# A list scheduler's costs set to other figures, and one sequence's depthwise convolution moved from VectorE and GpSimd to TensorE

## The chip, the cores and the metric

The kernel runs on the 8 cores of one Trainium2 chip. Each core computes two of the 16 sequences by itself, and the cores exchange nothing. The metric is the device time in microseconds of the slowest core, and the time of a kernel is the median of its runs.

## The reference, cut to what matters

One encoder layer, float32, `x` of (16, 2048, 1024). A pre-RMSNorm and one input projection give q, k, v, and two 512-wide branches `xl` and `gl`. Group A is softmax attention (8 query heads, 2 key/value heads of 64, rotary positions, no mask). Group B is the recurrent block whose first step the change touches:

```python
def centred_depthwise_conv(x, w, b):
    # x (B,S,C), w (CONV_WIDTH, C); taps at offsets -1, 0, +1, +2
    xp = jnp.pad(x, ((0, 0), (1, 2), (0, 0)))
    out = b[None, None, :]
    for j in range(CONV_WIDTH):          # 4 taps
        out = out + xp[:, j:j + S, :] * w[j][None, None, :]
```

The convolved `xc` feeds two block-diagonal gate products for each direction (sigmoids), a decay, and a scan forward and one backward over the 2048 tokens. Their sum times GeLU(`gl`) is the output of group B. Both groups are RMS-normalised, pass one output projection into the residual, and a SwiGLU feed-forward (1024 to 2816 to 1024) follows.

## The kernel before

A core holds everything transposed, channels in the 128 partitions and tokens along the free dimension, mostly in pieces of 512 tokens. The program records operations in streams, one list per purpose, and a list scheduler written in Python (`Prog.order`, lines 107 to 275) then fixes the order of the instructions on every engine. It plays the program through with each operation's `cost` and `lat` (all in us), the `nbytes` of its transfer and the free PSUM banks, and it takes what could start first on an engine. Ties on TensorE go by `pe_rank` (line 1066), and on the other engines a bias is added to the time at which an operation became ready (line 1069). `emit` then writes each engine's list in that order with the semaphore waits. So a `cost` has no effect on how long an instruction takes; it only changes the order. Engines run their lists strictly in order.

The streams of a core, with n = 0, 1 for the sequence:

- A0, A1 (`rec_A`, line 547): four chunks of 512 tokens each. Squares for the norm (line 571, ring `xsq` of 4), the normalised input `uT` (line 582), then 14 projections of 8 matmuls (`mm`, line 483). Query and key blocks have their own norm and rotary steps (lines 605 to 633; the queries leave through the ring `qst` of 4). `xl` and `gl` go through `stg` to the DRAM scratch `xl_d`, `gl_d` (lines 667 and 673).
- C0, C1 (`rec_C`, line 789): for each of 4 channel blocks `cc` and each half `h` of the sequence, `xlp` (one buffer) is loaded from `xl_d` by SyncE (lines 795 and 799). GpSimd makes the first tap with the bias (line 802), VectorE adds the three others (line 807), GpSimd casts to bf16 (line 811). Then gate matmuls, Tanh (line 820), Exp (823), a square on GpSimd (827), two VectorE products (829, 838), Sqrt (833), the scans (843), the sum (852), the product with `gl` (854) and a store to `lr_d`.
- B0, B1 (`rec_B`, line 707): attention in 256 steps for each sequence, each of two 64-row score matmuls (line 731), one Exp over 1024 columns on ScalarE (line 738) and two matmuls with V (line 770). The first `single` steps (`NS0` = 192 for sequence 0, 0 for sequence 1) issue scores one step at a time, the others two steps in one burst. Attention is held back until all of A0 and A1 is issued (line 135).
- D0 to D7: output projection (`d_out`), gate and up products (`d_gu`) and down product (`d_down`, line 1013) for 8 chunks of 512 tokens. The bf16 weights come from DRAM scratch, which the first chunk fills. `wdb` holds two, later four, tiles of w_down of [128, 22, 128] each, loaded at line 908.

PSUM has 8 banks. While attention runs, the scheduler leaves other work two of them (6 and 7), and before that all.

## Time and profile before

| what | value |
|---|---|
| runs of the kernel | 2007.98, 2010.20, 2259.01 us; median 2010.2 us |
| the profiled execution | 2000.34 us |
| span in it, slowest core (core 7) | 1998.8 us; the cores lie from 1983.7 to 1998.8 us |
| TensorE busy | 1785.9 us (89%), 8168 matmuls, mean granted clock 0.951 |
| VectorE busy | 1016.1 us (51%) |
| ScalarE busy | 1098.6 us (55%) |
| GpSimd busy | 350.8 us (18%) |

The busy time of TensorE counts matmuls as they overlap and at the clock that was granted (1.00 is 2.4 GHz, 0.50 is 1.2 GHz), so it isn't the time they would need at full speed. An average over the span hides that the stages have different limits. All times of stretches below are from the first instruction of core 7. "L483 <- ACT L820" is idle time of the engine before an instruction of line 483 that ended when one of line 820 finished.

### The profile page before, as it was taken

To read this page: it belongs to the slowest core of one execution; us is meant where nothing else is said; L and a number is where in the kernel's file an instruction comes from. 1 tells how busy PE (TensorE), PEld (TensorE's weight loads), DVE (VectorE), ACT (ScalarE), POOL (GpSimd) and SP (SyncE) were. 2 spreads that over 40 slices of the span, in tenths; PEclk is the share of its full clock that TensorE was granted. 3 is DMA by queue.
4 is the path that set the end of the run, shared out by engine and by line. 5 is a ranking of instruction groups with operands and counts; after the bars stand their busy time and mean duration, and the time that the engine had idled before them with its cause. 6 is when DMAs were issued, how large, how long until landed. Compare 5 with 4: busy or idle time off the path is not lost.

```text
span 1998.8 us, 24285 instructions; the slowest of 8 cores (1983.7 to 1998.8 us)
## 1 busy us (share of the span) xinstructions
PE 1785.9 (89%) x8168; PEld 714.0 (36%) x8168; DVE 1016.1 (51%) x1249; ACT 1098.6 (55%) x1372; POOL 350.8 (18%) x380
## 2 busy tenths in 40 slices
PE   6995666866769999999999999999999999999997
PEld 2442222311213333333333334444444444444443
DVE  3476999956794232315122253473454634545231
ACT  4678788799988877867677771232113212132010
POOL 2123656454341222100000000000000000000000
PEclk9997768988879999999999999999999999999999
DMA  8655233482318667557533246577486674664632
GB/s 192 190 171 155 95 119 108 129 211 85 98 54 216 135 149 169 133 155 194 152 91 86 85 141 206 162 208 230 142 250 187 189 237 150 196 198 132 215 107 100
DMA packets 139782, 310.97 MB, mean 156 GB/s; under 512 B 18544, under 2 KB 26864, under 8 KB 139664
## 3 DMA queue, kind: packets, MB, share of 16 engines
q1 hardware_dynamic: 111632, 228.55, 38.9%
q0 software_dynamic: 28032, 80.86, 15.7%
q8 instruction: 72, 1.18, 0.2%
q14 instruction: 46, 0.38, 0.1%
HBM read 263.05 MB, written 69.99 MB: 167 GB/s over the span
## 4 chain that ended last, share of the span: by engine, by line
PE 70%; ACT 9%; DVE 9%; DMA 5%; issue 4%; POOL 2%; SPq 0%; DVEq 0%; POOLq 0%; ACTq 0%
PE ps_all L483 56%; PE ps_all L770 9%; PE ps_all L731 5%; ACT arena L738 3%; DVE arena L843 2%; ACT arena L820 2%; DVE arena L807 1%; DMA arena<-q_d 1%; DMA xl_d<-arena 1%; DVE arena L838 1%; DVE arena L582 1%; DMA arena<-w_in 1%; POOL arena L802 1%; DVE arena L829 1%; ACT arena L833 1%
## 5 line engine op out<-in xcount | busy, mean ns | idle before, releaser
L483 PE MATMUL ps_all<-arena 128*128 128x512 bf16 (+1 forms) x6120 | 1462.1, 379 | 138.9 <-ACT arena L820 43.9
L483 PEld LDWEIGHTS ps_all<-arena 128*128 128x128 bf16 x6120 | 595.0, 100 | 860.5 <-issue 255.5
L738 ACT ACTIVATE arena<-ps_all 128x1024 bf16<-128x1024 f32 x512 | 503.2, 1029 | 149.6 <-PE ps_all L731 126.5
L770 PE MATMUL ps_all<-arena 128*65 128x512 bf16 x1024 | 389.7, 400 | 14.6 <-DVE arena L746 11.8
L1004 ACT ACTIVATE arena<-ps_all 128x512 f32<-128x512 f32 x176 | 105.2, 598 | 517.1 <-PE ps_all L483 516.8
L1006 DVE SCALAR_TENSOR_TENSOR arena<-arena,ps_all 128x512 f32<-128x512 f32 x176 | 120.9, 687 | 362.5 <-ACT arena L1004 361.9
L731 PE MATMUL ps_all<-arena 64*128 64x512 bf16 x1024 | 178.5, 395 | 50.3 <-ACT arena L738 46.1
L1027 POOL DMA_DIRECT2D outT<-arena x64 | 34.6, 540 | 1003.4 <-DVE arena L1025 996.6
L1009 DVE SCALAR_TENSOR_TENSOR arena<-arena,ps_all 128x512 bf16<-128x512 f32 x176 | 120.7, 687 | 130.9 <-PE ps_all L483 127.4
L770 PEld LDWEIGHTS ps_all<-arena 128*65 128x65 bf16 x1024 | 108.2, 112 | 211.8 <-issue 155.6
L1025 DVE TENSOR_TENSOR arena<-ps_all,arena 128x512 f32<-128x512 f32 x64 | 43.9, 689 | 154.3 <-PE ps_all L483 154.3
L731 PEld LDWEIGHTS ps_all<-arena 64*128 64x128 bf16 x1024 | 39.7, 94 | 202.8 <-issue 202.8
L827 POOL TENSOR_TENSOR arena<-arena 128x1024 f32<-128x1024 f32 x32 | 83.1, 2598 | 91.0 <-ACT arena L823 77.3
L820 ACT ACTIVATE arena<-ps_all,arena 128x512 f32<-128x512 f32 x128 | 83.7, 708 | 17.0 <-DVE arena L843 11.8
L957 DVE TENSOR_TENSOR arena<-arena 128x512 f32<-128x512 f32 (+1 forms) x104 | 74.7, 719 | 27.6 <-ACT arena L950 21.5
L807 DVE SCALAR_TENSOR_TENSOR arena<-arena 128x1024 f32<-128x1024 f32 x48 | 76.6, 1597 | 19.8 <-POOL arena L802 19.5
L843 DVE TENSOR_TENSOR_SCAN arena<-arena 128x1024 f32<-128x1024 f32 x32 | 82.7, 2599 | 0.1
L982 DVE TENSOR_TENSOR arena<-ps_all,arena 128x512 f32<-128x512 f32 x64 | 43.7, 689 | 57.6 <-PE ps_all L483 57.2
L950 ACT ACTIVATE arena<-arena 128x512 f32<-128x512 f32 x64 | 40.2, 630 | 59.3 <-DVE arena L982 58.6
L746 DVE COPY arena<-ps_all 65x1024 f32<-65x1024 f32 x32 | 38.9, 1217 | 63.5 <-PE ps_all L770 63.5
L829 DVE SCALAR_TENSOR_TENSOR arena<-arena 128x1024 f32<-128x1024 f32 x32 | 45.8, 1434 | 24.0 <-ACT arena L820 24.0
L973 DVE SCALAR_TENSOR_TENSOR arena<-arena 128x512 bf16<-128x512 bf16 x64 | 45.9, 779 | 23.7 <-ACT arena L490 23.6
(59 smaller groups left out, 996.9 us busy)
## 6 DMA issues: line engine op xcount, KB each, us to landing
arena<-wg_s SPq DMA_DIRECT2D x154, 256.0 KB, 3.0
arena<-wu_s SPq DMA_DIRECT2D x154, 256.0 KB, 3.1
arena<-wd_s SPq DMA_DIRECT2D x56, 704.0 KB, 5.4
arena<-xT SPq DMA_DIRECT2D x64, 512.0 KB, 7.5
outT<-arena POOLq DMA_DIRECT2D x64, 256.0 KB, 5.5
arena<-wo_s SPq DMA_DIRECT2D x56, 256.0 KB, 2.7
xl_d<-arena POOLq DMA_DIRECT2D x32, 256.0 KB, 4.6
gl_d<-arena POOLq DMA_DIRECT2D x32, 256.0 KB, 3.5
```

Source lines behind the costliest of these rows:

```text
L483: P.op("pe", lambda e: e.matmul(t.ap(n) if ap is None else ap(t), lhsT=lhsT, rhs=rhs, start=start, stop=stop), reads=reads, writes=[t], co ...
L731: r = e.matmul(T2[i].ap(1024)[:, u * 512:(u + 1) * 512], lhsT=kT[sq][rows, kt:kt + 128], rhs=qb[n % 2][rows, :], start=True, stop=True)
L738: P.op("act", lambda e, i=i, b=b: e.activation(out=Pb[b], in_=T2[i].ap(1024), func=AF.Exp, scale=0.125), reads=[T2[i]], writes=[("Pb", b)] ...
L770: P.op("pe", lambda e, u=u, V=V: e.matmul(O.ap(1024)[0:65, u * 512:(u + 1) * 512], lhsT=V[:, stl, :], rhs=pb[:, u * 512:(u + 1) * 512], st ...
L807: P.op("dve", lambda e, cc=cc, h=h, jj=jj: e.scalar_tensor_tensor(out=xc[h], in0=xlp[:, 2 * h + jj:2 * h + jj + 1024], scalar=col(PR, C_CW ...
L820: P.op("act", lambda e, GT=GT, dst=dst, bc=bc, sm=sm, cc=cc, qs=qs: e.activation(out=dst[:, qs], in_=GT.ap(), func=AF.Tanh, bias=col(DV, b ...
L827: P.op("pool", lambda e, u=u: e.tensor_tensor(out=us[u], in0=ua[u], in1=ua[u], op=ALU.mult), reads=[("ua", u)], writes=[("us", u)], cost=c ...
L843: P.op("dve", lambda e, u=u, rev=rev, init=init: e.tensor_tensor_scan(out=us[u][:, rev], data0=ua[u][:, rev], data1=ut[u][:, rev], initial ...
L957: P.op("dve", lambda e, o=o, sb=sb: e.tensor_tensor(out=o, in0=acc[a], in1=hsq[sb], op=ALU.add), reads=[("acc", a), ("hsq", sb)], writes=[ ...
L1004: P.op("act", lambda e, G=G, b=b: e.activation(out=tg[b], in_=G.ap(), func=AF.Tanh, scale=0.5), reads=[G], writes=[("tg", b)], cost=c_act( ...
L1006: P.op("dve", lambda e, G=G, b=b: e.scalar_tensor_tensor(out=tg[b], in0=tg[b], scalar=1.0, in1=G.ap(), op0=ALU.add, op1=ALU.mult), reads=[ ...
L1009: P.op("dve", lambda e, U=U, b=b, fc=fc: e.scalar_tensor_tensor(out=ffT[:, fc, :], in0=tg[b], scalar=0.5, in1=U.ap(), op0=ALU.mult, op1=AL ...
```

## The change

1. Costs in the scheduler: `c_act` from 0.085 + n/1200 to 0.18 + n/1220; several costs of `rec_A` and `rec_C` are replaced by other figures. No instruction changes by this, only the order.
2. Convolution of sequence 0 (stream C0): a new input `cdiag` holds for each channel block four diagonal 128x128 matrices in float32, one per tap. They are loaded into `cdg` (one buffer), four f32 matmuls of 512 columns with `xlp` at shifts 0 to 3 add up in one PSUM bank, and one VectorE instruction adds the bias and writes 512 columns of `xc`. Sequence 1 keeps the old form. `xsq` and `qst` give up one buffer of four each to make room for `cdg`.
3. `wdb` is cut into half tiles of [128, 11, 128], twice as many, each with a load of its own.
4. `down_last`: the first gate and up matmuls of a chunk are recorded after the first matmul of the last down product before them.
5. `NS0` from 192 to 256: all of sequence 0's attention issues scores one step at a time.
6. Streams D0 to D7 get a bias of -0.5 on the engines other than TensorE.

```diff
@@ costs @@
 def c_act(n, ptrs=0):
-    return 0.085 + n / 1200.0 + 0.09 * ptrs
+    return 0.18 + n / 1220.0 + 0.09 * ptrs
@@ rec_A @@
-        xsq = [RA.alloc([128, 512], BF16) for _ in range(4)]
+        xsq = [RA.alloc([128, 512], BF16) for _ in range(3)]
-        qst = [RA.alloc([128, 512], BF16) for _ in range(4)]
+        qst = [RA.alloc([128, 512], BF16) for _ in range(3)]
+        cdg = RA.alloc([128, 4, 128], F32)
...
-                         reads=[Z, ("rope", tc % 2)], writes=["t2b"], cost=c_dve(512))
+                         reads=[Z, ("rope", tc % 2)], writes=["t2b"], cost=0.9)
@@ rec_C @@
+                    if sq == 0:
+                        if h == 0:
+                            P.op("sp", lambda e, cc=cc: e.dma_start(out=cdg, in_=cdiag[cc]),
+                                 reads=[("xld", sq, 0, 0)], writes=["cdg"], dma="cdg", cost=0.4, nbytes=262144)
+                        for q in range(2):
+                            XC = misc()
+                            for jj in range(4):
+                                t0 = 2 * h + jj + q * 512
+                                mm(XC, cdg[:, jj, :], xlp[:, t0:t0 + 512], jj == 0, jj == 3, ["cdg", "xlp"],
+                                   cost=0.87)
+                            P.op("dve", lambda e, XC=XC, h=h, q=q, cc=cc: e.tensor_scalar(
+                                out=xc[h][:, q * 512:q * 512 + 512], in0=XC.ap(), scalar1=col(PR, C_CB + cc),
+                                scalar2=None, op0=ALU.add), reads=[XC, "PR"], writes=[("xc", h)], cost=0.68)
+                    else:
...
-                        reads=["xlp", "PR"], writes=[("xc", h)], cost=1.7, after=holds[cc])
+                            reads=["xlp", "PR"], writes=[("xc", h)], cost=2.2, after=holds[cc])
...
-                            cost=c_dve(1024) + 0.1)
+                                cost=1.6)
-                         reads=[("xc", h)], writes=[("xcb", h)], cost=1.7)
+                         reads=[("xc", h)], writes=[("xcb", h)], cost=1.5)
...
-                        reads=[("ut", u), ("xc", h)], writes=[("ut", u)], cost=c_dve(1024))
+                        reads=[("ut", u), ("xc", h)], writes=[("ut", u)], cost=1.43)
...
-                        reads=[("ua", u), ("ut", u)] + ([] if n < 2 else [("us", prev)]), writes=[("us", u)], cost=2.4)
+                        reads=[("ua", u), ("ut", u)] + ([] if n < 2 else [("us", prev)]), writes=[("us", u)], cost=2.6)
...
-                         reads=[("us", (1, h))], writes=[("us", (0, h))], cost=c_pool(1024))
+                         reads=[("us", (1, h))], writes=[("us", (0, h))], cost=3.1)
@@ streams D @@
-        wdb = [RD.alloc([128, NFC, 128], BF16) for _ in range(NWD)]
+        wdb = [RD.alloc([128, NFC // 2, 128], BF16) for _ in range(2 * NWD)]
...
-                        mm(T, wr[sl][:, k, :], u2T[:, k, :], k == 0, k == 7, [("wr", sl), ("u2", k)])
+                        mm(T, wr[sl][:, k, :], u2T[:, k, :], k == 0, k == 7, [("wr", sl), ("u2", k)],
+                           after=down_last if k == 0 else ())
...
+                sls = []
+                for hf in range(2):
+                    sl = dc["d"] % dc["nd"]
+                    dc["d"] += 1
+                    cols = slice(hf * 1408, hf * 1408 + 1408)
+                    w_load(g, wdb[sl], ("wdb", sl), "wd%d" % sl, w_down[:, cols], wd_s[:, cols], "wds%d" % hf, oc)
+                    sls.append(sl)
...
-        NS0 = 192
+        NS0 = 256
...
-        out = P.order(pe_rank, {"K": -9.0, "A0": -2.0, "C0": -1.0})
+        out = P.order(pe_rank, dict({"K": -9.0, "A0": -2.0, "C0": -1.0}, **{"D%d" % g: -0.5 for g in range(8)}))
```

The key `cdg` also joins `A_KEYS`, so the D buffers that lie on it wait for its last reader.

## Rows read from the trace of the kernel before

**Rows 1.** The page's busy tenths in 40 slices, each 50 us.
```profile
PE   6995666866769999999999999999999999999997
...
DVE  3476999956794232315122253473454634545231
ACT  4678788799988877867677771232113212132010
...
PEclk9997768988879999999999999999999999999999
```

**Rows 2.** Stretches: length, busy PE, PEld, DVE, ACT, POOL; clock, DMA, GB/s.
```profile
50.00:100.00 50.00, 45.79 (x247) 21.22 (x246) 24.48 (x38) 31.80 (x56) 8.96 (x17) 0.97 0.66 189
100.00:150.00 50.00, 46.93 (x233) 21.70 (x232) 37.42 (x55) 36.76 (x61) 13.01 (x22) 0.97 0.60 172
150.00:400.00 250.00, 166.69 (x699) 65.47 (x696) 228.68 (x198) 202.00 (x273) 135.37 (x93) 0.80 0.37 121
400.00:610.00 210.00, 139.99 (x516) 39.51 (x515) 153.67 (x110) 197.82 (x223) 92.53 (x58) 0.83 0.42 114
610.00:720.00 110.00, 105.61 (x478) 34.62 (x476) 40.29 (x57) 88.01 (x97) 20.27 (x38) 0.98 0.74 174
720.00:1200.00 480.00, 462.56 (x2231) 163.38 (x2230) 144.94 (x206) 352.27 (x391) 38.76 (x73) 1.00 0.52 135
1200.00:1960.00 760.00, 758.83 (x3516) 343.09 (x3515) 361.60 (x543) 167.44 (x237) 25.36 (x47) 1.00 0.61 185
```

**Rows 3.** TensorE's waits, 0 to 400 us (total, times, longest).
```profile
PE ps_all L483 <- ACT arena L820: 38.5, 21, 11.9
...
PE ps_all L483 <- DVE arena L624: 13.4, 7, 4.1
```

**Rows 4.** TensorE's waits, 400 to 600 us.
```profile
PE ps_all L731 <- ACT arena L738: 39.2, 37, 5.2
```

**Rows 5.** TensorE's waits, 1200 us to the end.
```profile
PE ps_all L483 <- DMA arena<-wd_s: 1.5, 1, 1.5
```

**Rows 6.** VectorE's groups by line, 150 to 400 us.
```profile
L807 DVE SCALAR_TENSOR_TENSOR arena<-arena 128x1024 f32<-128x1024 f32 x25 | 43.7, 1748 | 6.8 <-POOL arena L802 6.8
L582 DVE SCALAR_TENSOR_TENSOR arena<-arena 128x512 bf16<-128x512 f32 x29 | 24.0, 893 | 0.0
L622 DVE TENSOR_TENSOR arena<-arena 128x512 f32<-128x512 bf16 x20 | 22.2, 1109 | 0.1
...
L632 DVE TENSOR_TENSOR arena<-arena 128x512 bf16<-128x512 f32 x17 | 19.0, 1120 | 0.3
...
L624 DVE TENSOR_TENSOR arena<-ps_all,arena 128x512 f32<-128x512 f32 x20 | 13.6, 679 | 0.0
...
L651 DVE CAST arena<-ps_all 128x256 bf16<-128x256 f32 x4 | 1.7, 418 | 6.8 <-ACT arena L647 6.8
```

**Rows 7.** VectorE's groups by line, 50 to 110 us.
```profile
L582 DVE SCALAR_TENSOR_TENSOR arena<-arena 128x512 bf16<-128x512 f32 x21 | 14.2, 746 | 6.3 <-ACT arena L490 6.3
...
L622 DVE TENSOR_TENSOR arena<-arena 128x512 f32<-128x512 bf16 x6 | 4.1, 688 | 0.1
```

**Rows 8.** GpSimd's groups by line, 150 to 400 us.
```profile
L827 POOL TENSOR_TENSOR arena<-arena 128x1024 f32<-128x1024 f32 x17 | 44.7, 2634 | 45.3 <-ACT arena L823 42.4 <-DVE arena L854 2.7
...
L802 POOL TENSOR_SCALAR arena<-arena 128x1024 f32<-128x1024 f32 x9 | 23.3, 2590 | 7.1 <-DVE arena L829 5.6 <-DMA arena<-xl_d 1.2
L811 POOL CAST arena<-arena 128x1024 bf16<-128x1024 f32 x8 | 13.9, 1738 | 5.2 <-DVE arena L807 3.9 <-PE ps_all L483 1.2
```

**Rows 9.** TensorE in one short stretch at half the clock.
```profile
290.00:294.00 4.00, 4.00 (x11) 1.39 (x10) 4.00 (x4) 3.99 (x6) 0.88 (x2) 0.50 0.00 0
```

**Rows 10.** SyncE's queue: waits over the whole span.
```profile
SPq L335 <- DVE arena L807: 79.3, 9, 22.0
```

**Rows 11.** Line 731 alone by stretch: score matmuls, single and in pairs.
```profile
610.00:710.00 100.00, 28.55 (x144) 7.10 (x144) 0.98 0.74 174
720.00:1200.00 480.00, 97.15 (x640) 19.13 (x640) 1.00 0.52 135
```

More of the change, by code:

```diff
@@ L416, in build @@
     cmat = din("cmat", [128, 3, 128])
+    cdiag = din("cdiag", [4, 128, 4, 128])
     rope = din("rope", [128, 2, S])
@@ L480, in misc, with mm @@
             return Bank(P, "m")
-        def mm(t, lhsT, rhs, start, stop, reads, n=512, ap=None):
-            P.op("pe", lambda e: e.matmul(t.ap(n) if ap is None else ap(t), lhsT=lhsT, rhs=rhs,
+        def mm(t, lhsT, rhs, start, stop, reads, n=512, ap=None, after=(), cost=None):
+            return P.op("pe", lambda e: e.matmul(t.ap(n) if ap is None else ap(t), lhsT=lhsT, rhs=rhs,
                                           start=start, stop=stop),
-                 reads=reads, writes=[t], cost=c_pe(n), lat=0.25)
+                        reads=reads, writes=[t], cost=cost or c_pe(n), lat=0.25, after=after)
         def rstd(t, scale, out, key):
@@ L533, in build @@
                   + [("uT", b, k) for b in range(2) for k in range(8)] + [("rope", b) for b in range(2)]
-                  + [("xsq", b) for b in range(4)]
+                  + [("xsq", b) for b in range(3)] + ["cdg"] + [("qst", b) for b in range(3)]
                   + [(n, b) for n in ("sqb", "rsb", "qnb") for b in range(2)]
-                  + [(n, b) for n in ("stg", "qst") for b in range(4)])
+                  + [(n, b) for n in ("stg",) for b in range(4)])
         def load_w_in(sqid):
@@ L569, in pro1 @@
                 for k in range(8):
-                    xk, b = ("xin", k // 2), k % 4
+                    xk, b = ("xin", k // 2), k % 3
                     sqid[k] = P.op("act", lambda e, k=k, b=b: e.activation(out=xsq[b], in_=xin[:, k, :], func=AF.Square),
@@ L838, in rec_C @@
                     P.op("dve", lambda e, u=u: e.tensor_tensor(out=ut[u], in0=ut[u], in1=us[u], op=ALU.mult),
-                         reads=[("ut", u), ("us", u)], writes=[("ut", u)], cost=c_dve(1024))
+                         reads=[("ut", u), ("us", u)], writes=[("ut", u)], cost=1.33)
                     rev = slice(None, None, -1) if sm else slice(None)
@@ L881, in build @@
         wr += [RL.alloc([128, 8, 128], BF16) for _ in range(6)]
-        wdb += [RL.alloc([128, NFC, 128], BF16) for _ in range(2)]
+        wdb += [RL.alloc([128, NFC // 2, 128], BF16) for _ in range(4)]
         tg += [RL.alloc([128, 512], F32) for _ in range(2)]
@@ L885, in build @@
                    + [("ff", f) for f in range(NFC)] + [("wr", i) for i in range(6)]
-                   + [("wdb", i) for i in range(2)] + [("rf", 0)]
+                   + [("wdb", i) for i in range(4)] + [("rf", 0)]
                    + [("tg", i) for i in range(2)] + [("hsq", 0), ("hsq", 1), ("acc", 0), ("accb", 0)]
@@ L890, in build @@
                   + [("wr", i) for i in range(6, 12)]
-                  + [("wdb", i) for i in range(2, 4)] + [("tg", i) for i in range(2, 4)])
+                  + [("wdb", i) for i in range(4, 8)] + [("tg", i) for i in range(2, 4)])
         C_KEYS = (["xlp", "halo", "zg", "lro"] + [(n, i) for n in ("xc", "xcb") for i in range(2)]
                   + [(n, u) for n in ("ua", "ut", "us") for u in UNITS])
-        dc = {"g": 0, "a": 0, "d": 0, "o": 0, "t": 0, "s": 0, "r": 0, "ng": 6, "nd": 2, "nt": 2}
+        dc = {"g": 0, "a": 0, "d": 0, "o": 0, "t": 0, "s": 0, "r": 0, "ng": 6, "nd": 4, "nt": 2}
         LATE = 1
+        down_last = []
         def w_load(g, buf, key, group, src, dst, dkey, n):
@@ L1131 @@
             prm[:, 26 + cc * 4 + j] = cw[j, cc * 128:(cc + 1) * 128]
+    cdg = np.zeros((4, 128, 4, 128), f32)
+    for cc in range(4):
+        for j in range(4):
+            cdg[cc, np.arange(128), j, np.arange(128)] = cw[j, cc * 128:(cc + 1) * 128]
     prm[:, 42:46] = np.asarray(conv_b, f32)[0].reshape(4, 128).T
@@ L1151 @@
         "w_down": _tiles(np.asarray(w_down, f32)[0], NFC).reshape(8 * 128, DFF),
-        "w_rgi": wrgi, "prm": prm, "cmat": cm, "rope": rope,
+        "w_rgi": wrgi, "prm": prm, "cmat": cm, "rope": rope, "cdiag": cdg,
     }
```

32 lines of the change are left out of this document (16 added, 16 removed).

## The prediction

> **What bounds the kernel now.** I read the slices of the page first, then the stretches, then what TensorE waits for in them, then the groups of VectorE, ScalarE and GpSimd in the stretch that has the slack. The slices [rows 1] show three stages: up to 400 us TensorE is 6 to 9 tenths busy and VectorE fills up; from 400 to 600 ScalarE is at 9; after 600 TensorE is at 9 until the end. The stretches [rows 2] say it in numbers. From 720 on TensorE is busy 462.56 of 480 and 758.83 of 760 us at a clock of 1.00, so nothing but TensorE's own work counts there. From 150 to 400 (sequence 0's recurrent block C0 and sequence 1's projections A1) VectorE is busy 228.68 of 250 us, ScalarE 202.00 and TensorE 166.69, at a clock of 0.80. From 400 to 610 (attention B0 beside C1) ScalarE has 197.82 of 210. The end is set by TensorE, and all work before 610 counts by the time at which the full stage can begin. The longest wait of the first stage is for C0: 38.5 us behind the gates' Tanh, which stand behind the whole chain of C0, and 13.4 us behind VectorE's rotary product [rows 3]. In the second stage it is ScalarE's own pace, 39.2 us [rows 4].
>
> A look at the size of an unmixed matmul: 3516 in 760 us is 0.216 us each [rows 2]. At half the clock 11 stand in 4.00 us, 0.36 us each with the ones cut at the edges [rows 9].
>
> **What the convolution takes off VectorE.** C0 has 4 blocks x 2 halves, so 8 GpSimd instructions of line 802 and 24 VectorE instructions of line 807 go. From 150 to 400 line 807 has 25 instructions of 1.748 us, 43.7 us in all [rows 6]. Some four of them are C1's, and 3 of C0's ran before 150. I take 38.5 us off. Added are 2 evictions per half, 16 in all, 14 of them in this stretch; the row nearest to them is line 624, which also reads PSUM, 0.679 us [rows 6], so 9.5 us. VectorE also runs slowly beside GpSimd: line 622 takes 1.109 us in this stretch and 0.688 us at 50 to 110 us, line 582 takes 0.893 against 0.746 [rows 6, 7]. Over 20 and 29 instructions that is 8.4 + 4.3 us, and line 632, of the same kind as 622, adds about 7 more, some 20 us. GpSimd's compute here is lines 827, 852, 802 and 811; 802 with 23.3 us [rows 8] is about a fifth of it, so 4 us come back. VectorE goes from 228.7 to 228.7 - 38.5 + 9.5 - 4 = 196 us.
>
> **What it puts on TensorE.** 4 x 2 x 2 x 4 = 64 matmuls on f32 operands. No row has one. From below it is a bf16 matmul, 0.216 us; from above it is the diff's own cost, 0.87 us, at half the clock, 1.74 us. I take 0.87, which is four times 0.216 and the only figure made for this instruction: 64 x 0.87 = 56 us, of which 56 matmuls or 49 us lie in the stretch. It is spare time only if TensorE has it. Its 166.69 us there are at a clock of 0.80. At full speed 697 matmuls of line 483, 4 x 32 = 128 of them with 128 columns (line 651 evicts four value blocks, [rows 6]), come to 569 x 0.216 + 128 x 0.054 = 130 us. With the new ones it is 179 us at full clock and 216 us at the clock of before. Where TensorE was busy 94% of the time the clock was 0.97, where it was busy 67% it was 0.80 [rows 2]; with more to do I expect about 0.9, so near 197 us.
>
> The Trainium skill bears on this price. FP8 and Floating Point Precision, TensorE Precision Notes: a true f32 product takes four passes through the array, so the sum by it would be 64 x 4 x 0.216 = 55 us, as the diff says. TensorE: Matmul & The Clock Gate, Weight-path perf modes, speaks against the change: f32 weights don't get the fast load. If each pass loaded weights in the open, that would be extra on each; no run here shows it yet. It is the third rival's mechanism.
>
> **How long the stretch becomes.** Afterwards ScalarE has 202, TensorE 197, VectorE 196 us, three engines level, and none is hidden by another. ScalarE's work doesn't change, and 202 us is the floor. In the second stage ScalarE reaches 94% (197.82 of 210), which would be 215 us here. With three chains that feed each other I take 90%, 225 us: a gain of 25 us where VectorE alone would promise 33. The stall that goes is the one behind line 807; what is late next is ScalarE's Tanh and Exp with their table loads.
>
> The path of one half of C0 is hardly shorter: before, line 802 at 2.59 and three of 1.748, 7.8 us to the cast; after, 8 matmuls and a last eviction, 7.0 + 0.7 us. The first half of C0 runs before 150, where TensorE is busy 46.93 of 50 us [rows 2], so its 7 us of matmuls are no spare time; half of them pushes the rest: +3 us.
>
> **The moved transfers.** SyncE's queue gets 4 loads of 256 KB into `cdg`. The load for the next block waits for the last matmul on the block before. Behind it in the queue are the next `xlp` load, which waits for the same matmuls, and A1's loads of x and rope. SyncE stood 79.3 us behind line 807 already, for the `xlp` loads [rows 10]; it now stands behind TensorE for the same halves. DMA is at 0.37 in this stretch [rows 2]. Cost 0; if it isn't hidden, one late `xin` delays A1 by a few us. `xsq` and `qst` with three buffers: 0, at most 3 us, since Squares and matmuls alternate.
>
> **NS0.** The last 64 steps of B0 run with single scores. Line 731 takes 28.55/144 = 0.198 us per matmul in the single form and 97.15/640 = 0.152 in pairs [rows 11]. 128 x 0.046 = +6 us, in a stretch where TensorE is busy 96%. Bound from below 0, if the smoother supply of ScalarE repays it; from above 10, if waits in PSUM of the first 110 us of that stretch (4.4 us idle, [rows 2]) come with it.
>
> **Halved w_down tiles and `down_last`.** From 1200 on TensorE waits for w_down 1.5 us in all [rows 5]. That is all there is to gain: -1.5. Twice the loads (112 more on SyncE) are hidden by TensorE's own 758.83 us; uncovered they cost some us.
>
> **New costs and the bias for D.** They move no duration. They can bring D0 forward into the second stage, where TensorE idles 70 us but ScalarE only 12; so from -12 to, by symmetry, +12. I take 0.
>
> **The sum.** -25 + 3 + 6 - 1.5 = -17.5 us against the profiled execution's own 2000.3 us (span 1998.8): 1982.8. The shown median, 2010.2, stands 9.9 above the profiled execution, so in terms of the median 2010.2 - 17.5 = 1993 us.
>
> **Rivals.** All in terms of the median.
> 1. More: the stretch falls to ScalarE's floor, 202 us (-48), and the order by measured costs also empties ScalarE's 12 us in the second stage. -48 - 12 + 7.5 = -52.5, 1958 us. For it: VectorE was the fullest engine, and the old cost of line 807 (1.3 us by c_dve + 0.1) was far under its 1.748. Against: ScalarE has never been above 95% in any stretch.
> 2. The convolution's relief doesn't come through: ScalarE and its table loads are the true limit of the stretch, VectorE's 29 us turn into idle. +3 + 6 - 1.5, 2018 us. For it: ScalarE is busy 95% in the next stage. Against: only 81% in this one.
> 3. Slower: TensorE becomes the bound of the first stage. At 1.74 us a matmul, by half clock or by weight loads in the open, the stretch holds 166.7 + 56 x 1.74 = 264 us of TensorE, at 94% 281 us: +31, and the first half of C0 adds 8 instead of 3, so +31 + 8 + 4.5 = +43.5, 2054 us. It turns the change into a loss from 1.1 us a matmul on: (166.7 + 56 x 1.1)/0.94 = 243 us, whose 7 us of gain go to the other terms. For it: the clock here was 0.80. Against: more work lifts the clock.
> 4. The new order is worse in the second stage, by 12 us or more, with the forecast's gain: 2005 to 2015.
>
> **Chances.** Forecast (1980 to 2005) 0.48; rival 1 0.17, rival 2 0.18, rival 3 0.08, rival 4 0.09. The range goes half way to rival 3, whose chance is small, and nearly all the way to rival 1: 1962 to 2025. A measurement of this kernel tells about 2%, 40 us, from no change. Faster by more than that needs 1970 or less, most of rival 1: 0.15. Slower needs over 2050, the upper half of rival 3: 0.05. The rest is 0.80.
>
> **What would show it.** VectorE's total falls from 1016 to about 984 us, GpSimd's from 351 to about 330, TensorE gains 56 us of busy time in f32 matmuls of 0.87 us spacing. The first attention matmul, now just before 400 us, comes at about 378. The slices of TensorE before it read 8 and 9 in place of 6, and the clock is higher. Line 731's mean in the last quarter of B0 stays near 0.20. From then on the profile is the same, shifted. The forecast is wrong if attention starts at 395 or later (rivals 2, 3), if the f32 matmuls are spaced over 1.1 us (rival 3), or if ScalarE's share before attention passes 94% (rival 1).

## The result

The changed kernel took 2035.9 us (median of 4 runs), and 1.012 times the kernel before, with an interval of 1.006 to 1.018. Compared once more on another chip it was 1.0138 (1.008 to 1.019). That second figure is high by one run: of its five, four took 2026 to 2032 us and one 2051, and the medians of the same runs are at 1.012. So of a difference to 1.0138 below, some 0.002 can be this one run. The prediction was 1993 us, 17.5 us faster: the sign was wrong and the time lies above the range of 1962 to 2025. By the prediction's own sign ("wrong if attention starts at 395 or later") it was wrong too: attention starts at 413 us. Two medians of before can't be compared directly (2134.6 us with this result against 2010.2 when the prediction was made); disturbed runs are among them, and the ratios leave those out.

The page's busy tenths of the changed kernel, which answer to [rows 1]:

```profile
PE   6988776956669999999899999999999999999998
...
DVE  3454999736795342212422352374373553535331
ACT  4567876688998878767766774121121211113010
...
PEclk9988887988778999999999999999999999999999
```

The stretches in the changed kernel (length; busy PE, PEld, DVE, ACT, POOL; clock, DMA, GB/s), which answer to [rows 2]. The limits of the later ones are moved with the stages:

```profile
50.00:100.00 50.00, 46.21 (x244) 21.72 (x243) 24.64 (x38) 29.64 (x50) 9.64 (x18) 0.97 0.69 182
100.00:150.00 50.00, 41.13 (x187) 18.15 (x185) 25.69 (x40) 29.14 (x48) 6.45 (x12) 0.90 0.52 154
150.00:400.00 250.00, 202.02 (x803) 85.71 (x802) 199.18 (x192) 182.79 (x257) 97.88 (x83) 0.88 0.38 121
400.00:630.00 230.00, 146.65 (x533) 40.91 (x531) 163.36 (x120) 199.91 (x231) 114.83 (x69) 0.78 0.39 109
630.00:740.00 110.00, 107.37 (x493) 35.72 (x492) 35.19 (x50) 89.72 (x99) 22.57 (x42) 1.00 0.77 180
740.00:1240.00 500.00, 484.81 (x2322) 174.09 (x2320) 159.85 (x227) 359.87 (x395) 46.29 (x87) 1.00 0.55 138
1240.00:1980.00 740.00, 733.63 (x3398) 330.60 (x3397) 350.20 (x529) 149.55 (x224) 23.73 (x44) 1.00 0.61 184
```

From 150 to 400 us the engines did what was predicted: VectorE 199 us (196 predicted, 228.68 before), TensorE 202 us (197 predicted, 166.69 before) at a clock of 0.88, ScalarE 183 us. And yet the stretch didn't shorten. All three idle about a fifth of it or more, where 90% was assumed. Two of the three later stages grew too.

To compare versions I cut each profile at three events and took the median of its eight cores. "1st" ends where the first attention Exp starts, "2nd" with the first residual addition of D0 (line 982 before, 999 after), "3rd" with the second chunk's last down product, "4th" with the span. The last column is the ratio of the timed runs to the kernel before, with its interval. Two profiles of the same changed kernel give 413 and 409 us for the first stage, and 1 us or less for the others; a difference in the first stage of 4 us or less says nothing.

```
version              1st   2nd   3rd   4th   span   ratio
before               402   197   630   761   1991   1
after (1st result)   413   210   627   771   2023   1.0122 (1.006 to 1.018)
after_again          409   209   626   771   2017   1.0138 (1.008 to 1.019)
two_xlp              414   210   626   771   2021   1.0101 (1.007 to 1.014)
no_conv              410   212   632   763   2017   1.0087 (1.006 to 1.012)
conv_only            403   203   632   763   2003   1.0024 (1.000 to 1.004)
old_costs            404   200   634   768   2006   1.0038 (1.002 to 1.006)
old_c_act            400   211   625   764   2002   1.0060 (1.003 to 1.009)
costs_only           396   204   738   753   2091   1.0489 (1.046 to 1.052)
costs_down_last      396   202   636   775   2010   1.0118 (1.007 to 1.017)
ns192                409   208   625   775   2022   1.0117 (1.010 to 1.014)
no_dbias             413   212   638   763   2027   1.0136 (1.011 to 1.016)
no_down_last         412   209   626   766   2017   1.0125 (1.010 to 1.015)
conv_c0_first        412   203   631   762   2009   1.0061 (1.004 to 1.008)
conv_from_cc1        409   202   631   762   2006   1.0053 (1.003 to 1.007)
conv_rings4          406   204   632   762   2003   1.0042 (1.003 to 1.006)
after_rings4         405   211   627   771   2015   1.0102 (1.009 to 1.012)
rings3_only          403   208   630   763   2004   1.0032 (1.001 to 1.005)
before_5ns           406   202   636   769   2012   1.0083 (1.006 to 1.010)
after_10ns           410   205   631   767   2014   1.0078 (1.006 to 1.010)
```

The changed kernel's span is 26 us longer than before (2017 against 1991): +7 in the first stage, +12 in the second, -4 in the third, +10 in the fourth. The last two are best read together, as +6: 18 more matmuls stand behind the cut between them (3496 against 3478, about 4 us), and TensorE idles 3 us more behind it. The cores differ too, though all run one program: in the kernel before the second stage takes 195 to 198 us on the eight, in the changed kernel 204 to 215. The expectations below count the times of events from a zero 8 us earlier than this table (410 us there is 402 here); their differences are the same. The repeat stood to show how far one version differs from itself:

> The changed kernel as it is, on the same chip as the three experiments beside it, so that they can be compared with it and not only with the kernel before. Expected: 1.01 to 1.015 times the kernel before, as in the first result (1.0122), and the same picture: SyncE standing some 40 us behind TensorE between 120 and 165 us, and the first attention Exp about 12 us later than in the kernel before.

The loss is there again, and SyncE's 40 us too. The first Exp came 7 us later than in the kernel before, not 12.

### The profile page after: what moved, and what is told of

The parts are those of the page before. It is cut to its first block, busy times and chain, and to the rows that moved or that the text cites. A ratio compares the mean times of both kernels' runs of the same rounds, so it can differ in the third digit from the quotient of the medians.

```text
span 2031.7 us, 24767 instructions; the slowest of 8 cores (2003.5 to 2031.7 us)
## 1 busy us (share of the span) xinstructions
PE 1833.8 (90%) x8296; PEld 737.8 (36%) x8296; DVE 985.3 (48%) x1241; ACT 1063.8 (52%) x1340; POOL 337.8 (17%) x388
## 4 chain that ended last, share of the span: by engine, by line
PE 70%; DVE 9%; DMA 7%; ACT 7%; issue 4%; POOL 3%; SPq 1%; ACTq 0%; POOLq 0%; DVEq 0%
PE ps_all L484 54%; PE ps_all L772 10%; PE ps_all L733 6%; DMA arena<-xT 2%; ACT arena L740 2%; DMA arena<-w_in 1%; DMA arena<-xl_d 1%; DVE arena L859 1%; DVE arena L584 1%; POOL arena L843 1%; ACT arena L836 1%; DVE arena L845 1%; DVE arena L823 1%; DVE arena L1007 1%; DVE arena L854 1%
## 5 line engine op out<-in xcount | busy, mean ns | idle before, releaser
L484 PE MATMUL ps_all<-arena 128*128 128x512 bf16 (+2 forms) x6248 | 1503.9, 383 | 134.4 <-POOL arena L827 28.1
L484 PEld LDWEIGHTS ps_all<-arena 128*128 128x128 bf16 (+1 forms) x6248 | 619.4, 102 | 871.2 <-issue 263.0
L772 PE MATMUL ps_all<-arena 128*65 128x512 bf16 x1024 | 394.8, 402 | 17.6 <-DVE arena L748 14.9
L733 PE MATMUL ps_all<-arena 64*128 64x512 bf16 x1024 | 184.3, 397 | 35.7 <-ACT arena L740 32.1
L836 ACT ACTIVATE arena<-ps_all,arena 128x512 f32<-128x512 f32 x128 | 82.8, 712 | 25.2 <-PE ps_all L484 22.2
L489 ACT ACTIVATE arena<-ps_all,arena 128x512 f32<-128x512 f32 x72 | 48.6, 686 | 76.1 <-PE ps_all L484 67.6
L859 DVE TENSOR_TENSOR_SCAN arena<-arena 128x1024 f32<-128x1024 f32 x32 | 78.6, 2475 | 0.2
L845 DVE SCALAR_TENSOR_TENSOR arena<-arena 128x1024 f32<-128x1024 f32 x32 | 59.2, 1858 | 16.5 <-ACT arena L836 16.5
L584 DVE SCALAR_TENSOR_TENSOR arena<-arena 128x512 bf16<-128x512 f32 x64 | 50.6, 860 | 28.8 <-ACT arena L491 28.8
```

The source lines that it names most:

```text
L484: return P.op("pe", lambda e: e.matmul(t.ap(n) if ap is None else ap(t), lhsT=lhsT, rhs=rhs, start=start, stop=stop), reads=reads, writes= ...
L733: r = e.matmul(T2[i].ap(1024)[:, u * 512:(u + 1) * 512], lhsT=kT[sq][rows, kt:kt + 128], rhs=qb[n % 2][rows, :], start=True, stop=True)
L772: P.op("pe", lambda e, u=u, V=V: e.matmul(O.ap(1024)[0:65, u * 512:(u + 1) * 512], lhsT=V[:, stl, :], rhs=pb[:, u * 512:(u + 1) * 512], st ...
L836: P.op("act", lambda e, GT=GT, dst=dst, bc=bc, sm=sm, cc=cc, qs=qs: e.activation(out=dst[:, qs], in_=GT.ap(), func=AF.Tanh, bias=col(DV, b ...
L845: P.op("dve", lambda e, u=u, h=h: e.scalar_tensor_tensor(out=ut[u], in0=ut[u], scalar=1.0, in1=xc[h], op0=ALU.add, op1=ALU.mult), reads=[( ...
L859: P.op("dve", lambda e, u=u, rev=rev, init=init: e.tensor_tensor_scan(out=us[u][:, rev], data0=ua[u][:, rev], data1=ut[u][:, rev], initial ...
```

## The experiments

### The convolution by itself

`conv_only` is the kernel before with part 2 of the change alone (with `cdg` and the rings of three). `no_conv` is the changed kernel without it:

```diff
-                    if sq == 0:
+                    if False:
                         if h == 0:
```

> The kernel before with the convolution of sequence 0 on TensorE alone (and cdg, and the three-buffer rings xsq and qst); all other costs, NS0, w_down tiles and biases as before. If the convolution costs time, this is 10 to 25 us slower than the kernel before, and attention begins 8 to 20 us later than there. If it gains, attention begins 10 to 30 us earlier and the time falls by about as much.

> The changed kernel with C0's convolution back on GpSimd and VectorE; the new costs, halved w_down tiles, down_last, NS0 and the D bias stay (the order is planned anew). If the convolution on TensorE is what costs the time, this is 10 to 25 us faster than the changed kernel and close to the kernel before. If it gains in the first stage, as I predicted, and the loss comes from the other parts, this is 10 to 25 us slower than the changed kernel. VectorE gets its 24 instructions of about 1.7 us back.

The convolution alone costs 0.24% (0.0 to 0.4), and its first stage is as long as before, 403 against 402 us. The gain of 25 us that I had predicted there isn't in any version: their first stages last 396 to 414 us, and 378 was predicted. Without the convolution the changed kernel is still at 1.0087, 4 to 10 us faster than with it, within the intervals. So most of the loss seems to lie elsewhere.

The price of the f32 matmul was right. TensorE's matmuls in a dense stretch of the changed kernel (171 to 177 us, clock 1.00), and its weight loads over the whole kernel, by shape:

```profile
L484 PE MATMUL ps_all<-arena 128*128 128x512 f32 x13 | 5.7, 591 | 0.0
L484 PE MATMUL ps_all<-arena 128*128 128x512 bf16 x3 | 0.8, 378 | 0.0
```

```profile
L484 PEld LDWEIGHTS ps_all<-arena 128*128 128x128 bf16 x6120 | 595.1, 100 | 842.1 <-issue 235.4
...
L484 PEld LDWEIGHTS ps_all<-arena 128*128 128x128 f32 x128 | 24.5, 200 | 29.1 <-issue 27.5
```

Each f32 matmul stands there as two records (128 for 64), 13 of them in 5.7 us, so 0.88 us for a matmul (0.87 predicted). Its weight load of 0.2 us is longer than bf16's 0.1, but in this stretch it stands beside the matmuls. The Trainium skill's FP8 and Floating Point Precision, TensorE Precision Notes (four passes), agrees: 0.88 is about four times 0.216. Its TensorE: Matmul & The Clock Gate, Weight-path perf modes (no fast load for f32), agrees as to the load's length; the cost I had feared from it isn't seen in this stretch.

### Does the head of C0 eat the gain?

In conv_only the first cast of C0 came at 157 us against 129 in the kernel before, since TensorE was full of A0 and A0 ranks above C0. Its stretches, core 7:

```profile
100.00:150.00 50.00, 45.75 (x225) 21.01 (x224) 29.79 (x46) 32.11 (x53) 12.56 (x24) 1.00 0.54 174
150.00:200.00 50.00, 42.38 (x150) 18.20 (x149) 24.47 (x24) 41.42 (x56) 15.54 (x12) 0.93 0.40 126
200.00:250.00 50.00, 37.80 (x111) 14.46 (x111) 49.93 (x46) 38.79 (x50) 26.07 (x14) 0.86 0.41 120
```

VectorE is at 24.47 of 50 us from 150 to 200, and full after that. Two versions of conv_only bring the head forward:

```diff
-            return {"K": 0, "A0": 0.5, "B0": 1, "A1": 2, "C0": 1.5, "C1": 3.2, "B1": 3.5}.get(s, 4)
+            return {"K": 0, "A0": 0.5, "B0": 1, "A1": 2, "C0": 0.4, "C1": 3.2, "B1": 3.5}.get(s, 4)
```

> The convolution alone on the kernel before (old costs), with C0 ahead of A0 in TensorE's ranks (0.4 in place of 1.5). In the convolution-only kernel the first bf16 cast of C0 came at 165 us against 136 before: the matmuls of its first half are spread from 141 to 163 us among A0's, and VectorE, which should have gained 29 us, idles meanwhile. Theory H (C0's late head eats the gain): with the rank turned the first cast comes at 140 to 150 us, attention begins 8 to 20 us earlier than 410, and the time is 0.4 to 1% below the convolution-only kernel (1.0024), so 0.992 to 0.998. Rival (the stage is limited by ScalarE and A1's chain, not by when C0 begins): the cast is early but attention begins at 405 us or later, ratio 1.000 or more.

```diff
-                    if sq == 0:
+                    if sq == 0 and cc > 0:
```

> The convolution alone on the kernel before, but C0's first channel block keeps the GpSimd and VectorE form, at the time when TensorE is full with A0 and VectorE isn't; the other three blocks go to TensorE. Theory H: C0 starts as early as before (first cast 136 us), VectorE has still 20 us less, and attention begins 8 to 20 us earlier than 410; ratio 0.992 to 0.998. Rival as in the run beside it: attention at 405 or later, ratio 1.000 or more.

The first cast came at 137 and 133 us, and attention began at 412 and 409 us, later than in conv_only. Theory H fell: an earlier C0 didn't bring attention forward in either order. Of its rival the half that names A1 is left, and the half that names ScalarE isn't: in conv_from_cc1 VectorE and ScalarE have slack in every 50 us after 200, and still the stage is long:

```profile
200.00:250.00 50.00, 32.50 (x86) 12.02 (x87) 41.63 (x33) 35.47 (x50) 27.77 (x12) 0.77 0.40 123
250.00:300.00 50.00, 39.20 (x127) 15.32 (x129) 45.49 (x39) 41.61 (x52) 24.43 (x17) 0.94 0.29 92
300.00:350.00 50.00, 39.55 (x176) 16.72 (x178) 37.52 (x38) 31.34 (x49) 19.67 (x18) 0.83 0.41 135
350.00:400.00 50.00, 48.63 (x260) 23.36 (x265) 36.17 (x53) 33.28 (x54) 14.74 (x26) 1.00 0.43 134
```

### SyncE's queue

In the changed kernel SyncE stood 39.8 us at one place behind TensorE (its queue's waits, 90 to 400 us), and A1's loads of rope and x stood behind it (its issues, 117 to 187 us):

```profile
SPq L335 <- PE ps_all L484: 80.2, 6, 39.8
```

```profile
164.62 0.34 SPq L801 DMA_DIRECT2D arena<-xl_d  x1
...
177.71 0.55 SPq L554 DMA_DIRECT2D arena<-rope  x1
186.59 4.39 SPq L561 DMA_DIRECT2D arena<-xT  x4
```

The same view of the kernel before has 57.0 us behind line 807, the longest 22.0. `two_xlp` gives C0's second halves a buffer of their own. Every engine's order stays what the planner made of the changed kernel (but for one memset more at the start); `loads` holds for each half its load and the matmuls that read it, and once the order stands, a load no longer depends on the matmuls of the half before, only on those of the half before that:

```diff
+        xlq = arena[:, RB_.start // 2:(RB_.start + 4120) // 2].bitcast(F32)
...
-                        P.op("sp", lambda e, cc=cc: e.dma_start(out=xlp[:, 2:1027], in_=xl_d[sq][cc, :, 1023:2048]),
+                        ld = P.op("sp", lambda e, cc=cc: e.dma_start(out=(xlp, xlq)[sq == 0][:, 2:1027], in_=xl_d[sq][cc, :, 1023:2048]),
...
+        for n in range(1, len(loads)):
+            d = P.ops[loads[n][0]]["deps"]
+            d.difference_update(loads[n - 1])
+            if n > 1:
+                d.update(loads[n - 2])
```

> The changed kernel with a second xlp buffer for C0's second halves (it lies on Pb, which is unused until attention), and with every engine's instruction order kept exactly. Only the wait of the xlp load on the convolution of the half before is gone. Theory Q (SyncE's queue stands behind TensorE at this load, and A1's rope and x loads behind it come late, which holds A1 back): the 39.8 us stand goes, A1's x loads come 20 to 35 us earlier and attention begins 8 to 20 us earlier, so 0.4 to 1% less time than the changed kernel. Rival L (the first stage is longer because TensorE has 56 us more work in it, and the loads are late only because nothing needs them): attention begins within 3 us of the changed kernel's, and the time is the same.

Its SyncE issues, and the wait in front of the first of them:

```profile
SPq L808 <- DMA xl_d<-arena: 32.1, 1, 32.1
```

```profile
155.79 0.34 SPq L808 DMA_DIRECT2D arena<-xl_d  x1
...
176.38 0.55 SPq L559 DMA_DIRECT2D arena<-rope  x1
185.26 4.39 SPq L566 DMA_DIRECT2D arena<-xT  x4
```

The `xlp` load of the second half went 9 us earlier, at 155.79, but the queue still stood 32.1 us in front of it, now for A0's last `xl` chunk in DRAM. The rope and x loads came at 176.38 and 185.26, 1 us earlier and not 20 to 35. Attention began at 414 us; the ratio, 1.0101, can't be told from 1.0138. So the wait on the convolution costs nothing, as the next wait is nearly as long. Whether A1 would gain from loads that come 20 us earlier was not tested by this.

### The costs

`old_costs` takes the changed kernel back to the costs of before, `old_c_act` only `c_act`, and `costs_only` puts the twelve new costs on the kernel before. The edit of `old_c_act`:

```diff
 def c_act(n, ptrs=0):
-    return 0.18 + n / 1220.0 + 0.09 * ptrs
+    return 0.085 + n / 1200.0 + 0.09 * ptrs
```

> The changed kernel with the scheduler's costs of before (c_act and the others that the change set), all else as changed: convolution on TensorE, halved w_down tiles, down_last, NS0 = 256, D bias. Two experiments left the first stage's 10 us open: it was as long without the convolution (first attention Exp at the median of the cores 419 us, 422 in the changed kernel, 410 before) and not longer with the convolution alone (410). Theory K (the new costs order the first stage worse): here the first Exp comes at 405 to 412 us, and the time falls to 1.000 to 1.008 times the kernel before. Rival (the three-buffer rings together with something else, not the costs): it stays at 418 or later and at 1.012 or more.

> The changed kernel with c_act alone back at 0.085 + n/1200; the measured VectorE and GpSimd costs stay. If c_act is the part that matters (it is in every pick of ScalarE, and sets what one table switch is worth), the time comes to 1.004 to 1.007 times the kernel before and ScalarE's busy share before attention rises. If the recurrent block's costs matter, it stays at 1.011 or more. In between, both do.

> The kernel before with the twelve new scheduler costs and nothing else. With the convolution in, going back to the old costs took the ratio to the kernel before from 1.0138 to 1.0038. If the costs alone are the loss, whatever the rest, this is 1.01 or more. By theory K it is at least that: first Exp at 414 us or later against 410, first residual addition of D0 10 to 20 us later. If the costs only hurt together with the convolution, it is within 1.003 of the kernel before.

The old costs recover 1.0% (1.0138 to 1.0038; 0.8% by medians), and the intervals lie apart, so going back to them removes the greater part of the loss. c_act alone gives 1.0060, as expected if it is the part that matters, but its interval (1.003 to 1.009) touches that of the changed kernel. Whether the size of the costs does it, or only that they make another order, these three runs don't tell. Theory K, a worse first stage, held for old_costs (404 us, from 409 or 413) and failed for costs_only: on the kernel before the new costs make the first stage 6 us shorter (396), and the third 108 us longer. The stretches of costs_only, core 4, and the groups from 1000 to 1200 us:

```profile
600.00:1000.00 400.00, 375.58 (x1764) 127.50 (x1762) 126.48 (x178) 302.37 (x332) 59.86 (x111) 1.00 0.66 159
1000.00:1200.00 200.00, 127.47 (x569) 30.96 (x568) 11.69 (x11) 137.40 (x143) 0.00 (x0) 0.97 0.08 18
```

```profile
L738 ACT ACTIVATE arena<-ps_all 128x1024 bf16<-128x1024 f32 x143 | 138.6, 1021 | 63.4 <-PE ps_all L731 63.4
L770 PE MATMUL ps_all<-arena 128*65 128x512 bf16 x285 | 89.4, 397 | 53.3 <-ACT arena L738 48.7 <-DVE arena L746 4.6
L731 PE MATMUL ps_all<-arena 64*128 64x512 bf16 x284 | 44.5, 389 | 19.2 <-ACT arena L738 19.2
```

The 569 matmuls are lines 770 and 731; line 483, and so every D stream, is absent for 200 us, while TensorE waits for the Exp. `costs_down_last` adds down_last to it:

```diff
                         mm(T, wr[sl][:, k, :], u2T[:, k, :], k == 0, k == 7, [("wr", sl), ("u2", k)],
+                           after=down_last if k == 0 else ())
```

> The kernel before with the new costs and down_last. With the costs alone no matmul of the D streams ran from 1000 to 1200 us, and D0's down products ended at 1218 us against 993. Theory B (with the new costs the scheduler starts D1's gate and up products ahead of D0's down products; their two banks then wait for ffT, which D0's down products still read, and those find no bank until attention is over): down_last forbids that order, D0's down products end at 990 to 1010 us and the ratio falls from 1.049 to 1.00 to 1.012. Rival (something else, the whole w_down tiles or NS0, keeps D0's down products back): it stays above 1.03.

Its stretch, core 7:

```profile
1000.00:1200.00 200.00, 194.68 (x942) 69.94 (x943) 59.75 (x84) 142.25 (x160) 1.08 (x2) 1.00 0.35 99
```

TensorE is full again, the third stage is 636 us, and D0's down products end at 977 us (986 before, 1211 in costs_only). That down_last forbids the bad order is shown; that the two banks were what held D0's down products is read from the code and not measured by itself. In the changed kernel itself, no_down_last didn't fall into the bad order (third stage 626 us), so there another part avoids it too; which one wasn't tried.

### The small parts

```diff
-        NS0 = 256
+        NS0 = 192
```

> The changed kernel with NS0 back at 192. By my term of the prediction, 64 steps with two score matmuls each 0.046 us dearer in the single form, this is 4 to 8 us faster than the changed kernel (ratio 1.009 to 1.011 where the changed kernel has 1.0138), all of it between the 192nd Exp and the end of the first sequence's attention. If the single form costs nothing, as ScalarE is supplied more evenly, the two are equal. The first stage stays as in the changed kernel.

Line 731's row in the changed kernel (now line 733), whose stretches answer to [rows 11]: from 740 to 850 us the single form, then pairs.

```profile
740.00:850.00 110.00, 30.62 (x158) 7.47 (x158) 1.00 0.65 143
860.00:1240.00 380.00, 72.51 (x480) 13.81 (x480) 1.00 0.51 136
```

That is 0.194 and 0.151 us per matmul, as in [rows 11]. ns192 gave 1.0117 against 1.0138, 4 us less, but inside the intervals; the medians of the runs show none of it, nor do its stages at one place. Unclear.

`no_dbias` and `no_down_last`, both on the changed kernel:

```diff
-        out = P.order(pe_rank, dict({"K": -9.0, "A0": -2.0, "C0": -1.0}, **{"D%d" % g: -0.5 for g in range(8)}))
+        out = P.order(pe_rank, {"K": -9.0, "A0": -2.0, "C0": -1.0})
```

```diff
-                           after=down_last if k == 0 else ())
+                           after=())
```

> The changed kernel without the bias of -0.5 for the streams D. Theory: the bias lets D0's work go ahead of the second sequence's recurrence on VectorE and ScalarE, so the second stage (first Exp to the first residual addition of D0, 211 us against 197 before) gets back to 200 us or less without it, and the time falls by 5 to 12 us. Rival: the stage's length comes from the costs; then it stays at 208 to 214 us and the time within 4 us of the changed kernel.

> The changed kernel without down_last (the halved w_down tiles stay). In the changed kernel the pure feed-forward stage has a chunk that takes 137 us in place of 131, with TensorE waiting for VectorE's sum of squares (5.1 us in all after 1250 us). If down_last causes it, by leaving no gate and up matmuls to put between, the waits go and the end comes 4 to 8 us earlier. If the costs cause it, nothing changes.

Without the bias the sum stays the same, and so does the second stage, 212 us, as the rival said. Without down_last the fourth stage is 5 us shorter. TensorE's waits in it, first of the changed kernel, then of no_down_last:

```profile
PE ps_all L484 <- DVE arena L974: 5.1, 4, 2.3
PE ps_all L484 <- DVE arena L1050: 0.8, 2, 0.6
```

```profile
PE ps_all L484 <- DVE arena L1050: 0.8, 2, 0.6
PE ps_all L484 <- DVE arena L1027: 0.3, 1, 0.3
```

The 5.1 us behind line 974, the sum of squares before the norm's matmul, are gone. The ratio, 1.0125, is too near to 1.0138 to confirm the 5 us by time.

### The rings of three

The cut from four buffers to three in `xsq` and `qst` was a part I had priced at nothing. `conv_rings4` and `after_rings4` keep four and put `cdg` where Pb's first buffer lies; `rings3_only` makes both rings three on the kernel before:

```diff
-        cdg = RA.alloc([128, 4, 128], F32)
+        cdg = arena[:, RB_.start // 2:RB_.start // 2 + 1024].bitcast(F32).rearrange("p (a b) -> p a b", a=4)
```

```diff
-        qst = [RA.alloc([128, 512], BF16) for _ in range(4)]
+        qst = [RA.alloc([128, 512], BF16) for _ in range(3)]
```

> The convolution alone on the kernel before (old costs), but xsq and qst keep four buffers; cdg lies on Pb's first buffer, unused until attention. Theory R (the rings cut to three eat the convolution's gain, since A1's squares and rotary products then wait for a buffer): attention begins at 395 to 404 us (410 with three), and the ratio falls from 1.0024 to 0.994 to 0.999. Rival (the first stage isn't held by these buffers): attention at 408 to 412, ratio 1.001 to 1.004.

> The whole change, but xsq and qst keep four buffers (cdg on Pb's first). Theory R: attention begins at 405 to 412 us in place of 418 to 422, and the ratio falls from 1.0138 to 1.004 to 1.010. Rival: within 0.002 of 1.0138.

> The kernel before with xsq and qst of three buffers and nothing else. Theory R: attention begins 5 to 15 us later than 410 and the ratio is 1.003 to 1.008. Rival: 408 to 413 us, ratio within 0.002 of 1.

In the changed kernel four buffers may help (1.0138 to 1.0102, attention 4 us earlier), but both lie within the spread of its repeats; conv_only they don't help (1.0024 to 1.0042). Three buffers alone cost the kernel before 0.3% (0.1 to 0.5), which is in theory R's range by luck: its first stage is 1 us longer and not 5 to 15, and the time goes in the second stage (208 us for 197), where neither ring is used. A wait for a buffer doesn't explain that. Another order may; the order did change, VectorE's at 305 of 1249 places.

### A change without meaning

`before_5ns` on the kernel before, `after_10ns` on the changed kernel:

```diff
-    return 0.085 + n / 1200.0 + 0.09 * ptrs
+    return 0.09 + n / 1200.0 + 0.09 * ptrs
```

```diff
-    return 0.18 + n / 1220.0 + 0.09 * ptrs
+    return 0.17 + n / 1220.0 + 0.09 * ptrs
```

> The kernel before with c_act 0.090 + n/1200 in place of 0.085 + n/1200: 5 ns more for each ScalarE operation, a change without meaning, since the real durations lie 40 to 90 ns above either. Theory F (the kernel before has an order that fits well among many, and any touch that reshuffles the list gives some of it back, mostly in the second stage): the second stage, 197 us in the kernel before and 200 to 212 in every other version so far, gets 200 to 210 us, and the ratio is 1.004 to 1.012. Rival M (what matters is the step to costs of another size): within 0.002 of 1.

> The changed kernel with c_act 0.17 + n/1220 in place of 0.18 + n/1220. Theory F: the stages shift by several us either way, and the ratio differs from 1.0138 by 0.002 to 0.006; by rival M it stays within 0.002 of it.

Five nanoseconds in one cost, on the kernel before, cost 0.83% (0.62 to 1.04), clear of noise. They changed the order: another line's instruction stands at 2100 of TensorE's 8168 places and at 573 of VectorE's 1249, and ScalarE has 16 table loads fewer. (By the traces the real durations lie some 80 to 130 ns above this cost, not 40 to 90.) The loss is spread over all four stages (+4, +5, +6, +8 us), not mostly over the second, as theory F had it; its ratio and its second stage (202 us) came out. Ten nanoseconds less on the changed kernel gave 1.0078, with a second stage of 205 in place of 209. That is theory F's 0.006, and beyond rival M's 0.002 also against the medians' 1.012, but its interval (1.006 to 1.010) and that of 1.0138 overlap. So costs of another size aren't needed to lose most of a per cent: a reshuffle did it once, on the kernel before.

## Why the prediction was wrong

**What bounds the kernel.** Right: the later stages are TensorE's, and the first two decide when they begin. What I took for the limit of the first stage, the level of busy time, was not it. The stage ends where attention may begin, and the program holds attention back until all of A1 is issued; C0 isn't in that condition.

**VectorE's relief.** Right in the changed kernel: 199 us for 196, and VectorE's total fell to 985 us for about 984. Part of that is luck. The 38.5 us taken off are 22 instructions of 1.748 us, where the text counts 21 (36.7), and in conv_only, with the convolution alone, VectorE has 209 us in the stretch. It also came in other lines than I had said. VectorE's groups of the changed kernel, 150 to 400 us, which answer to [rows 6]:

```profile
L845 DVE SCALAR_TENSOR_TENSOR arena<-arena 128x1024 f32<-128x1024 f32 x16 | 32.2, 2026 | 8.0 <-ACT arena L836 8.0
...
L624 DVE TENSOR_TENSOR arena<-arena 128x512 f32<-128x512 bf16 x21 | 14.4, 687 | 0.4
...
L634 DVE TENSOR_TENSOR arena<-arena 128x512 bf16<-128x512 f32 x17 | 12.9, 758 | 0.2
L814 DVE TENSOR_SCALAR arena<-ps_all,arena 128x512 f32<-128x512 f32 x15 | 11.1, 740 | 14.6 <-PE ps_all L484 12.4 <-POOL arena L843 2.1
```

The old line 622 (here 624) fell from 1.109 us to 0.687, and 632 (634) from 1.120 to 0.758, while 829 (845) rose from about 1.3 to 2.0. The eviction took 0.740 us, where 0.68 was assumed.

**TensorE's load.** Right: 202 us for 197, clock 0.88 for 0.9, 0.88 us a matmul.

**How long the stretch becomes: this step failed.** "With three chains that feed each other I take 90%, 225 us." VectorE, TensorE and ScalarE fell to 80, 81 and 73% of an unchanged stretch: the term of -25 us came out at 0 with the convolution alone (403 us for 402) and at +7 with the whole change. Taking work off the fullest engine bought nothing. In conv_only the last half block of C0 is cast at 295 us for 325 before, and the last of A1's projections is evicted at 396 for 395 (medians of the cores): C0 did get faster, A1 didn't, and attention waits for A1. So C0 was not what ended the stage. A1 even ran late: the normalised inputs of its four chunks (line 582, there 584) were ready at 182, 214, 310 and 351 us, before at 150, 190, 268 and 331. From 355 to 395 us TensorE is then full (39.40 of 40 us on core 7, clock 1.00), so a later last input can't be made up. What makes A1 late is open. VectorE is still full from 200 to 250 us (49.93 of 50), and the planner gives C0 a bias of -1.0 there and A1 none; no version without that bias was run. Rival 2 had the right effect (relief that turns into idle) for the wrong reason: ScalarE was no fuller than before, 201 us in conv_only and 183 in the changed kernel.

**"New costs and the bias for D. They move no duration ... I take 0": this step failed too, and as far as one order for each version tells, it is behind most of the slower time.** I bounded it by 12 us in the second stage alone. Going back to the old costs the runs put it at 1.0%, 16 to 20 us; in the profiles the first stage gets 5 us shorter, the second 9, the fourth 3, and the third 8 longer (against after_again). The bias by itself did nothing. Rival 4 (a worse second stage, 12 us or more) named what happened to that stage: 197 to 209 us, with the gain it assumed beside it missing. TensorE's waits there, 400 to 600 us, which answer to [rows 4]:

```profile
PE ps_all L733 <- ACT arena L740: 25.9, 28, 4.0
PE ps_all L484 <- POOL arena L827: 24.2, 5, 10.0
PE ps_all L772 <- DVE arena L748: 11.5, 3, 5.9
```

A wait of 24.2 us stands behind GpSimd's cast of C1. It isn't the common cause: before_5ns, whose second stage is longer too (202 us), has 5.6 us there. The same view of the kernel before has less than half of it, behind the same line (then 811):

```profile
PE ps_all L483 <- POOL arena L811: 9.7, 3, 5.4
```

**NS0**: the price per matmul was right, its 6 us couldn't be told by time. **Halved w_down tiles and down_last**: the 1.5 us of [rows 5] went, and 5.1 us behind line 974 came (the loads are 112 for 56, so 56 more and not 112); I had looked for what down_last spares and not for what it leaves TensorE to do while a norm is computed. **The moved transfers**: nothing contradicts the cost of 0, and two_xlp shows that SyncE's 40 us at the convolution cost nothing by themselves. **The rings**: "0, at most 3 us" was too little on the kernel before, where three buffers alone cost 0.3%, 6 us; in the other two versions their price isn't clear of noise.

What stays open is which property of the order makes the second stage 197 us in the kernel before and 200 to 212 in all the others. All 18 other versions had it longer, the one with 5 ns too. I read that as the kernel before holding a good draw among many orders. The change without meaning supports it, one draw on each kernel, and doesn't prove it. If it is so, an edit to such a list is likely to lose some tenths of a per cent before its own merit counts, and that holds for the single runs above as well: each compares two orders, and only two_xlp kept the order. No version tried beats the kernel before.

## What to carry to other kernels

Where a list scheduler fixes the order, a price for "costs only, no duration changes" is not zero: perturb one cost by a few nanoseconds first and measure how far the time moves, since that is the noise under every other edit. Here one such change cost 0.8%. Compare edits with the order frozen where the dependencies allow it, as in two_xlp, or over several orders. Busy time of 80 to 90% on three engines at once is no promise that relief of the fullest one shortens a stage; look at which stream's last operation ends it, and what that stream waits for.

## What the runs showed that I had not expected

An f32 matmul of 128x128 with 512 columns appears as two records of 0.44 us spacing at full clock, and its weight loads take 0.20 us each against 0.10 for bf16. VectorE's f32 product on SBUF operands (line 622, then 624) took 1.109 us on average from 150 to 400 us in the kernel before and 0.687 in the changed kernel, although GpSimd was still busy 98 of the 250 us. The traces of all eight cores show where it is slow. Where no GpSimd computation overlaps it, it takes 0.673 to 0.694 us in both kernels. Where one does, it takes 0.66 to 2.84 us, 1.52 on average in the kernel before. There 66 of 320 overlap, in the changed kernel 15 of 320. So what counts is how they fall together, and GpSimd's sum of busy time doesn't tell it. Fewer table loads didn't help either: ScalarE made 106 of them in the kernel before and 74 in the changed one, had 35 us less to do in all, and the time was longer.
